# Recurrent-branch norm: from a full-width Sqrt and reciprocal to one variance per token and head, raised to -0.5 on POOL and spread by products

## Reference

```python
y = rwkv7_scan(r, decay, k, v, kk, a)
mu = jnp.mean(y, axis=-1, keepdims=True)
var = jnp.mean(jnp.square(y - mu), axis=-1, keepdims=True)
y = (y - mu) * lax.rsqrt(var + GN_EPS) * gn_g.astype(f32) + gn_b.astype(f32)
y = y + jnp.sum(r * k * r_k.astype(f32), axis=-1, keepdims=True) * v
y = y.reshape(B, T, RWKV_WIDTH).astype(gate.dtype)
return y * jax.nn.silu(gate)
```

## Time and profile before

| | us |
|---|---|
| median of 3 runs (lowest, highest) | 4830.44 (4821.56, 4830.96) |
| the profiled execution | 4825.16 |
| its span, first to last instruction | 4823.4 |
| busy in it: PE, DVE, ACT, POOL | 4165.9, 2781.7, 2156.7, 1162.6 |
| the phase of scan and attention, in the span | about 870 to 2412 |
| store of the last norm block (issue) | 2320.3 |

### The profile page before, as it was taken

One profiled execution on the slowest core, in us unless ns is written; L12 is line 12 of the kernel. 1 busy time (PEld: TensorE's weight loads), 2 busy tenths in 40 slices (PEclk: granted clock), 3 DMA queues, 4 the chain that ended last, 5 costly groups with the idle time before them and its releaser, 6 DMA issues. The chain is left out here.

```text
span 4823.4 us, 78905 instructions
## 1 busy us (share of the span) xinstructions
PE 4165.9 (86%) x32376; PEld 2814.8 (58%) x32376; DVE 2781.7 (58%) x5074; ACT 2156.7 (45%) x3170; POOL 1162.6 (24%) x919
## 2 busy tenths in 40 slices
PE   7998997768778877778678999798999999999879
PEld 6766765455555655556357788674444444444457
DVE  5556554557677767777564322345666666666443
ACT  4444443767777567776433322221233332333431
POOL 1111110253233434333111000001333333343200
PEclk9999998879889888888689999897999999999989
DMA  3333333112111111121066533663322323222143
GB/s 126 101 112 109 94 101 119 39 30 46 29 29 37 44 33 35 38 51 30 26 195 192 183 132 102 226 224 66 67 54 66 72 54 73 56 54 58 43 156 112
DMA packets 390601, 411.62 MB, mean 85 GB/s; under 512 B 116640, under 2 KB 288352, under 8 KB 389984
## 3 DMA queue, kind: packets, MB, share of 16 engines
q1 hardware_dynamic: 388144, 399.59, 28.8%
q10 hardware_dynamic: 2096, 6.99, 0.4%
HBM read 254.85 MB, written 151.62 MB: 84 GB/s over the span
## 5 line engine op out<-in xcount | busy, mean ns | idle before, releaser
L142 ACT ACTIVATE PT<-psum 128x1024 f32<-128x1024 f32 x384 | 372.2, 1021 | 896.4 <-PE psum L132 896.4
L170 DVE TENSOR_REDUCE m<-psum 128x1 f32<-128x1024 f32 x384 | 469.9, 1224 | 439.2 <-PE psum L132 439.0
L132 PE MATMUL psum<-xc,wah 128*128 128x512 f32 x1600 | 513.7, 402 | 1.5 <-DVE xc L146 1.5
L146 POOL TENSOR_TENSOR part<-PT 128x1024 f32<-128x1024 f32 x144 | 342.7, 2380 | 639.9 <-DVE all L146 445.6
L132 PE MATMUL psum<-PT,V 128*64 128x512 f32 x1536 | 370.5, 603 | 0.2 <-ACT PT L142 0.2
L143 ACT ACTIVATE bias<-score,cand,cols 128x2048 bf16<-128x2048 f32 (+6 forms) x217 | 314.3, 1448 | 114.5 <-DVE cand L158 111.1
L146 POOL TENSOR_TENSOR Lm<-gm,cst 64x512 f32<-64x512 f32 x192 | 257.8, 1343 | 412.5 <-PE psum L132 253.7
L143 ACT ACTIVATE sgn<-score,cand,cols 128x1920 bf16<-128x1920 f32 (+6 forms) x217 | 290.8, 1340 | 133.4 <-DVE cand L158 132.0
L132 PEld LDWEIGHTS psum<-xc,wah 128*128 128x128 f32 x1600 | 299.6, 190 | 77.3 <-issue 9.2
L132 PE MATMUL psum<-hc,w4h 128*128 128x512 f32 x1024 | 320.4, 394 | 11.6 <-ACT w4h L142 11.6
L132 PE MATMUL psum<-xc,wal 128*128 128x512 f32 x800 | 315.8, 395 | 0.0
(11 more groups left out here) (337 smaller groups left out, 9184.0 us busy)
## 6 DMA issues: line engine op xcount, KB each, us to landing
raw_a<-in_w_a SPq DMA_DIRECT2D x50, 512.0 KB, 4.0
raw_w<-in_w_in SPq DMA_DIRECT2D x32, 512.0 KB, 4.5
QNh<-scr_qnh SPq DMA_DIRECT2D x48, 256.0 KB, 5.0
QRh<-scr_qrh SPq DMA_DIRECT2D x96, 128.0 KB, 4.9
QNl<-scr_qnl SPq DMA_DIRECT2D x48, 256.0 KB, 7.1
QRl<-scr_qrl SPq DMA_DIRECT2D x96, 128.0 KB, 6.3
xin<-in_x SPq DMA_DIRECT2D x16, 512.0 KB, 3.5
scr_AR<-AR SPq DMA_DIRECT2D x32, 256.0 KB, 2.5
```

The lines of the kernel that those rows point to most:

```text
L132: return self.e.matmul(out, a, b, start=start, stop=stop, skip_group_check=True)
L142: return self.e.activation(out, src, f, bias=bias, scale=scale)
L146: return self.e.tensor_tensor(out, a, b, op) if self.e else self.vector(out)
L170: return self.e.tensor_reduce(out, a, AX, op, negate=negate) if self.e else self.vector(a)
```

## The change

The sum over a head is now taken with tokens on partitions. `gn1` makes four products on PE, in which the squares `y2[:, h, :]` are the weights and `heads_of` (two columns of `blk`, one for each head) is streamed: they give 128 tokens x 8 heads in 8 columns of `bank[2]`. DVE scales these 8 columns and adds the epsilon into a new tile `iv`, and POOL raises `iv` to the power -0.5. A new piece `gn2` spreads the result back over the features on PE: eight products with one column of `iv`, broadcast to 64, as weights, and the identity streamed. DVE multiplies `yc` by `bank[2]`. The Sqrt on ACT, the reciprocal on DVE and the 128x512 product on POOL are gone; gain, offset, bonus and gate stay on POOL.

```diff
-        epg = sb("epg", [128, 1])
+        iv = sb("iv", [128, 8])
+        heads_of = blk.rearrange("p (a b) -> p a b", a=2)[:, :, 0]
...
-                    "sc": 2.0, "gn0": 3.0, "gn1": 5.0, "kT": 0.9, "vv": 0.9}.get(what, 0.4)
+                    "sc": 2.0, "gn0": 3.0, "gn1": 2.0, "gn2": 4.0, "kT": 0.9, "vv": 0.9}.get(what, 0.4)
...
-                b2 = {"lv0": (i_act, "xl"), "lvy": (i_act, "y"), "gn0": (s_dve, "yc"), "gn1": (s_act, "gn")}[k[0]] + k[1:]
+                b2 = {"lv0": (i_act, "xl"), "lvy": (i_act, "y"), "gn0": (s_dve, "yc"), "gn1": (s_dve, "gv"),
+                      "gn2": (s_dve, "yn")}[k[0]] + k[1:]
...
+                    elif what == "gn1":
+                        q.wait_ge(s_act, "y2", i)
+                        for h in range(4):
+                            t = q.mm(bank[2][:, 2 * h:2 * h + 2], y2[:, h, :], heads_of)
+                        t.then_inc(*s_pe.up("gn1", i))
                     else:
-                        q.wait_ge(s_act, "y2", i)
-                        q.mm(bank[2], blk, y2[:, :, :]).then_inc(*s_pe.up("gn1", i))
+                        q.wait_ge(s_pool, "iv", i)
+                        for h in range(4):
+                            for e in range(2):
+                                t = q.mm(bank[2][64 * e:64 * e + 64, 128 * h:128 * h + 128],
+                                         iv[:, 2 * h + e:2 * h + e + 1].broadcast_to([128, 64]), ident)
+                        t.then_inc(*s_pe.up("gn2", i))
...
-                elif what == "gn1":
-                    i = k[1]
-                    q.wait_ge(s_pool, "epg")
-                    q.wait_ge(s_pe, "gn1", i)
-                    q.act(y2[:, :, :], quads(bank[2]), ACT.Sqrt, bias=epg[:, :], scale=1.0 / 64).then_inc(*s_act.up("gn", i))
...
-                    q.wait_ge(s_act, "gn", i)
-                    q.recip(y2[:, :, :], y2[:, :, :]).then_inc(*s_dve.up("iv", i))
+                    q.wait_ge(s_pe, "gn1", i)
+                    q.wait_ge(s_pe, "gn2", i - 1)
+                    q.ts(iv[:, :], bank[2][:, 0:8], 1.0 / 64, 64e-5, ALU.mult, ALU.add).then_inc(*s_dve.up("gv", i))
+                elif what == "gn2":
+                    i = k[1]
+                    q.wait_ge(s_pe, "gn2", i)
+                    q.wait_ge(s_dve, "yc", i)
+                    q.tt(yc[:, :, :], yc[:, :, :], quads(bank[2]), ALU.mult).then_inc(*s_dve.up("yn", i))
...
-                    q.wait_ge(s_dve, "iv", i)
+                    q.wait_ge(s_dve, "gv", i)
+                    q.tt(iv[:, :], iv[:, :], neghalf[:, 0:8], ALU.pow).then_inc(*s_pool.up("iv", i))
+                elif what == "gn2":
+                    i = k[1]
+                    q.wait_ge(s_dve, "yn", i)
                     q.wait_ge(p_dve, "half")
-                    q.tt(yc[:, :, :], yc[:, :, :], y2[:, :, :], ALU.mult).then_inc(*s_pool.up("yn", i))
-                    q.wait_ge(s_pool, "yn", i)
```

More of the change, by code:

```diff
@@ L1072, in seq_pieces @@
                 out += [("sm", i, c), ("sa", i, c)] + [("yout", i - 1) if c == 0 else ("lds", i)] + [("sb", i, c), ("sc", i, c)]
-            return [k for k in out if k != ("yout", -1)] + [("gn0", i), ("gn1", i)]
+            return [k for k in out if k != ("yout", -1)] + [("gn0", i), ("gn1", i), ("gn2", i)]
         rwkv_order = []
@@ L1145, in program @@
         for k in rwkv_order:
-            if k[0] in ("lv0", "lvy", "gn0", "gn1"):
+            if k[0] in ("lv0", "lvy", "gn0", "gn1", "gn2"):
                 b2_free[k] = b2
-                b2 = {"lv0": (i_act, "xl"), "lvy": (i_act, "y"), "gn0": (s_dve, "yc"), "gn1": (s_act, "gn")}[k[0]] + k[1:]
+                b2 = {"lv0": (i_act, "xl"), "lvy": (i_act, "y"), "gn0": (s_dve, "yc"), "gn1": (s_dve, "gv"),
+                      "gn2": (s_dve, "yn")}[k[0]] + k[1:]
         pvs = {k[1:]: n for n, k in enumerate(k for k in dsa_order if k[0] == "pv")}
@@ L1169, in lane_2 @@
             return {"ld": "inverse", "gram": "inverse", "lv0": "inverse", "lvy": "inverse", "lvl": "inverse", "lvu": "inverse", "gn0": "norm",
-                    "gn1": "norm", "yout": "norm", "kT": "kv", "vv": "kv", "qd": "scores", "score": "scores", "exp": "scores", "pT": "values",
+                    "gn1": "norm", "gn2": "norm", "yout": "norm", "kT": "kv", "vv": "kv", "qd": "scores", "score": "scores", "exp": "scores", "pT": "values",
                     "pv": "values", "rb": "values", "fin": "values"}.get(what, "chunks")
@@ L1353, in pe_2 @@
                     t.then_inc(*s_pe.up("y", i, c))
-                elif what in ("gn0", "gn1"):
+                elif what in ("gn0", "gn1", "gn2"):
                     i = k[1]
@@ L1710, in pool_2 @@
         def pool_2(q):
-            q.fill(epg[:, :], 64e-5).then_inc(*s_pool.up("epg"))
             q.fill(Z[0][:, :, :], 0.0).then_inc(*s_pool.up("z0"))
@@ L1715, in pool_2 @@
                 what = k[0]
-                if what in ("gn1", "log", "nobias", "eq", "tie"):
+                if what in ("gn1", "gn2", "log", "nobias", "eq", "tie"):
                     q.wait_ge(i_pool, "lm", *halves)
```

## The result

The changed kernel takes 4743.85 us (median of 4 runs, 4739.77 to 4748.33) against 4830.70 of before (4 runs): a ratio of 0.9825, 95% interval 0.981 to 0.9841, 87 us less. The forecast was 15 us less.

A forecast was written before the change was run, and what follows sets the result against it. No engine is full; four engines in fixed orders handing each other small pieces bound the phase. Weighting PE by half, ACT and DVE by a quarter each gave -15 us: 4830.4 - 15 = 4815 us, range 4792 to 4843.

The forecast's parts named there:

- The order: Planner's new order for all engines of the phase: sign unreadable from any row, 10 us to either side, put into the range.
- ACT, a quarter's say, -11 us: ACT in the phase: Sqrt and 28 table loads go, 46.9 us of 1068 given up, weighted by a quarter.
- DVE, a quarter's say, -9 us: DVE in the phase: reciprocal goes, two smaller operations come, 39.4 us of 1054 given up, weighted by a quarter.
- Count (c): PE's queue only: 18.9 us of waits behind reciprocals and table loads return, 24.7 us work added; phase +6 us.
- PE, half the say, +16 us: PE in the phase: new gn1 and gn2 products less the old one add 24.7 us (11 to 34), weighted by half.
- POOL: POOL's power of 8 columns taken at 2.9 us (0.6 to 4.7), replacing a 1.387 us product; no cost where POOL is free.
- The rival in which PE waits for POOL: `gn2` on PE waits for a late power, 4.6 us in six blocks, 28 us in all: slower, 4843 us; chance 0.22.
- The tail: Phase's end, 2320 to 2412 us: short attention pieces without norm, so relief might not reach the end.

The follow-up runs named there:

- run 1: Kernel before, only SP's order changed: a block's own loads (bt, wu) ahead of the next block's inverse loads (ar, bk); 4775.35 us, ratio 0.9883.
- run 2: Changed kernel with SP's order turned back: the next block's inverse loads ahead of the block's own loads; 4811.49 us, ratio 0.9957.
- run 5: Kernel before in its own order, Sqrt replaced by a Square needing no table load, reciprocal kept; 4828.85 us, ratio 0.999.
- run 6: Kernel before in its own order, reciprocal replaced by a two-scalar operation, Sqrt and table loads kept; 4795.50 us, ratio 0.9923.
- run 7: Changed kernel in its order, the twelve products of gn1 and gn2 issued twice; 4761.37 us, ratio 0.9852.
- run 10: Changed kernel with the power on POOL replaced by a multiplication of the same 8 columns; 4737.24 us, ratio 0.98.
- run 9: Changed kernel in its order, a 512-column reciprocal put back on DVE ahead of the 8-column operation; 4790.79 us, ratio 0.9916.
- run 12: Changed kernel with a block's loads split by chunk on SP, every other engine keeping the changed kernel's order; 4711.65 us, ratio 0.9752.
- run 11: Kernel before, norm unchanged, with a block's own loads ahead of the next block's on SP and split by chunk; 4767.09 us, ratio 0.9866.

## Why the prediction was wrong

The step that failed is "The order. ... Its sign can't be read from any row; I give it 10 us to either side". On SP it could be read. The largest DMA row of PE's waits was there, 56.4 us for `wu` in 15 blocks, and the two orders of SP's queue show the loads that PE waits for moved ahead of four other issues in the changed kernel. The orders of PE and POOL stand ahead of the prediction, that of the queue that this row names does not; the prediction only listed a change of that wait among what would make it wrong. The term is worth 56 us (run 1) to 67 us (run 2), and without it the changed kernel is 20 us faster than before, where 15 were forecast.

That the rest came close is luck: ACT's term was too large, DVE's too small, and a term was missing. Point by point:

- *ACT, a quarter's say, -11 us.* The 46.9 us were given up as counted, but taking the table loads away moved the time by some 5 us, 10 at most by the interval (run 5). PE's waits for ACT in the earlier trace rows gave no price for it either: releasing PE earlier there only let it wait elsewhere, as the waits of run 5 show, where DMA's row for `wu` grew from 56.4 to 61.8 us.
- *DVE, a quarter's say, -9 us.* The size, 39.4 against 40.0 measured, was right, the weight was not: without the reciprocal the kernel before is 37 us faster (run 6), 0.8 us for each us. DVE's queue carries the round of the threshold search and the copies that free PSUM for PE, and 3.3 us is the longest block in it. Count (c) took only the waits of PE within two us behind a reciprocal, 9.7 us; of PE's waits for DVE 21 us went in run 6, so the delay comes out later too.
- *PE, half the say, +16 us.* 24.7 us was mis-sized, 18.8 measured, since a record with 128 columns of weights and two streamed takes 17.6/128 = 0.138 us, between the bounds 0.078 and 0.184. About half of such time is paid (run 7), some 8 us; the half was right within the run's uncertainty.
- *POOL.* 1.70 us, between 0.6 and 2.9. The rival in which PE waits for POOL did not come: 0.09 us is the longest that PE was idle ahead of `cst,iv`, and run 10 agrees.
- *`bank[2]`, missing from the sum.* The norm now hands the bank over three times, and DVE does each of the reads; the prediction put this at nothing. PE's waits for it went from 0.7 to 17.5 us, and in run 9, where 42 us were added to them, each us of them cost about a us of time.
- *The tail.* No norm was in it, as said; the whole phase moved forward ahead of it.

By these rates the change without SP's order is an estimated -37 (DVE) - 5 (ACT) + 8 (PE) + 17 (`bank[2]`) = -17 us, against the 20 of run 2. The first term is rather large, as run 6 took 46.8 us off DVE and the change 40.0. What the rest of the new order does within that was not measured apart. The split is worth 32 us in the changed kernel (run 12), where it took 24.5 us of wait for `wu`, and some 8 in the kernel before (run 11), where it took 10.3; how much of this difference is the order planned for run 11 stays open.

## What to carry to other kernels

Where a planner writes the order, compare the order of every queue before forecasting, the DMA issuer's above all, and start with the queue that the longest DMA row among the waits names: a tie broken otherwise on SP was worth three times what the rest of the change gave. Do not give engines a say by their busy share: a relief is worth what stands behind it in that queue, some 5 us of 36 on ACT here and 37 of 47 on DVE. Count the hand-overs of a shared PSUM bank, and ask what stands ahead of the read that frees it. And ask of each load whether the waiting instruction needs all of it: letting the first product wait for two loads in place of seven gave 32 us more where 25 us of wait were left, and some 8 where 12.5 were.

## What the hardware showed that was not expected

PE's busy time in the phase falls when its waits fall, with the same products or more: 1169 us at a granted clock of 0.85 before, 1161 at 0.87 in the changed kernel with 18.8 us of added work, 1131 at 0.90 with the loads split. A us of PE's waiting for `wu` that went brought more than a us in three of four pairs: 44 us less gave 56 us (run 1), 56 us more cost 67 (run 2), 24.5 less gave 32 (run 12); in run 11 10.3 less gave some 8. That the clock is the reason was not tested. And seven DMA issues (`bt` and `wu`) take SP 4.3 to 6.7 us in the two timelines above.
